# Half of a value projection moved from before attention into its filler steps, with the split weights in three rotating places

## What is computed

```python
h = x + 0.5 * swiglu(rmsnorm(x, g_ffn1), w1g, w1u, w1d)     # D_FF 2816
u = rmsnorm(h, g_mix)
qa, ka, va, qb, kb, vb = split(u @ w_in)                    # 512 128 128 512 512 512 columns
qa, ka, qb, kb = rope(...)
oa = sliding window attention with sinks(qa, ka, va)        # 8 q heads, 2 kv heads, hd 64
ob = differential attention(qb, kb, vb, lam)                # 4 heads of two 64-wide maps, 128-wide values
h = h + concat(oa, rmsnorm(ob, g_subln) * (1 - lam_init)) @ w_out
h = h + 0.5 * swiglu(rmsnorm(h, g_ffn2), w2g, w2u, w2d)
y = rmsnorm(h, final_norm)          # new keys and values are outputs too
```

## Time and profile before

| | |
|---|---|
| three runs | 1102.89, 1105.26, 1105.74 us; median 1105.26 |
| the profiled execution | 1108.34 us, its span 1106.5 us |
| TensorE | busy 97% of the span, 7890 products, mean granted clock 0.987 |
| VectorE, ScalarE, GpSimd | 62%, 43%, 8% |
| value projection | 422.8 to 458.0 us, 240 products |
| attention with fillers | 458 to some 675 us |

### The profile page before, as it was taken

How to read it: one execution, slowest core, us unless ns; L and a number is a source line. 1 busy time by engine, 2 the same in 40 slices (tenths; PEclk the granted TensorE clock), 3 DMA queues, 4 the chain that set the end, 5 groups by cost and what they waited for, 6 DMA issues and landing times. The chain is left out here.

```text
span 1106.5 us, 19039 instructions
## 1 busy us (share of the span) xinstructions
PE 1075.0 (97%) x7890; PEld 1043.7 (94%) x7890; DVE 689.4 (62%) x1083; ACT 475.1 (43%) x817; POOL 87.3 (8%) x84
## 2 busy tenths in 40 slices
PE   9999999999999999999999898999999999999996
PEld 8999999999999999877788778999999999999996
DVE  6898742488874333556678765599872268886323
ACT  6536521265653233333335443454552135655222
POOL 0000000000000213022222102100000000000112
PEclk9999999999999999989999998999999999999998
DMA  5233223223222224300111211132322323222202
GB/s 203 77 119 111 77 82 97 99 87 115 77 79 86 85 98 144 128 21 1 49 60 56 86 43 58 58 123 88 102 80 80 102 77 115 77 103 79 79 27 86
DMA packets 22660, 94.43 MB, mean 85 GB/s; under 512 B 2928, under 2 KB 6000, under 8 KB 18096
## 3 DMA queue, kind: packets, MB, share of 16 engines
q1 hardware_dynamic: 22576, 93.23, 25.0%
HBM read 88.24 MB, written 4.98 MB: 84 GB/s over the span
## 5 line engine op out<-in xcount | busy, mean ns | idle before, releaser
L1458 DVE TENSOR_TENSOR w_lo<-raw,w_hi 128x1024 fp32r<-128x1024 f32 (+3 forms) x145 | 177.1, 1221 | 208.4 <-ACT w_hi L1086 208.1
L750 PE MATMUL acc<-c_hi,w_lo 128*128 128x288 f32 x952 | 282.0, 296 | 0.0
L750 PE MATMUL acc<-c_hi,w_hi 128*128 128x288 f32 x952 | 280.9, 295 | 0.0
L750 PE MATMUL acc<-c_lo,w_hi 128*128 128x288 f32 x952 | 277.6, 292 | 0.0
L670 PE MATMUL acc<-h_hi,w_hi 128*128 128x288 f32 x1024 | 222.2, 296 | 1.0 <-DVE w_lo L1458 1.0
L670 PE MATMUL acc<-h_lo,w_hi 128*128 128x288 f32 x1024 | 221.1, 295 | 0.0
L670 PE MATMUL acc<-h_hi,w_lo 128*128 128x288 f32 x1024 | 221.0, 295 | 0.0
L1086 ACT ACTIVATE w_hi<-raw 128x1024 fp32r<-128x1024 f32 (+3 forms) x145 | 149.1, 1028 | 166.1 <-PE acc L670 147.8
L750 PEld LDWEIGHTS acc<-c_lo,w_hi 128*128 128x128 f32 x952 | 180.8, 190 | 0.0
L750 PEld LDWEIGHTS acc<-c_hi,w_hi 128*128 128x128 f32 x952 | 178.9, 188 | 0.0
L750 PEld LDWEIGHTS acc<-c_hi,w_lo 128*128 128x128 f32 x952 | 178.5, 187 | 0.0
(11 more groups left out here) (207 smaller groups left out, 1300.9 us busy)
## 6 DMA issues: line engine op xcount, KB each, us to landing
raw<-in_w1gu SPq DMA_DIRECT2D x17, 1024.0 KB, 4.8
raw<-in_w2gu SPq DMA_DIRECT2D x17, 1024.0 KB, 4.8
raw<-in_w1d SPq DMA_DIRECT2D x16, 704.0 KB, 4.0
raw<-in_w2d SPq DMA_DIRECT2D x16, 704.0 KB, 4.1
raw<-in_w_qk SPq DMA_DIRECT2D x13, 512.0 KB, 3.6
raw<-in_w1gu SPq DMA_DIRECT2D x10, 512.0 KB, 4.2
raw<-in_w2gu SPq DMA_DIRECT2D x10, 512.0 KB, 3.7
raw<-in_w_out SPq DMA_DIRECT2D x8, 512.0 KB, 4.1
```

The lines of the kernel that those rows point to most:

```text
L750: m = nc.tensor.matmul(acc[:, banks[side(f)], 0:HALF], w_part[:, col:col + P], x_part[:, k, c, :], start=n in (P1, P5, P2) and k == 0 and ...
L1458: return nc.vector.tensor_tensor(cols, src, hi.bitcast(FP32), ALU.subtract).then_inc(split_ready, 1)
```

## The change

The second half of the value projection leaves its place ahead of attention. It becomes 20 filler steps (`VALUES`, `value_step`) of two rows' blocks, six products of 320 columns each, placed in the list of fillers behind the sixth tile (kb0) and ahead of the seventh. Its token tiles alternate between banks 0 and 1; its first step waits for the take-out of the sixth tile, its third to fifth token tile for the eviction two before, and the seventh tile's first step for all ten evictions. The first scores wait for the first half's five. The loads and splits follow: the third tile comes directly behind the first two value blocks, and the other two value blocks behind the sixth tile (`FIRST_BLOCKS`, `MIDDLE`). In `w_hi` and `w_lo`, three places that begin at 0, 1280 and 2560 take turns throughout this part and in the plain gate and up blocks; the down blocks keep their two. The stores of new values move behind the eleventh tile's load. ScalarE evicts the second half in the course of the list. The lists of the order are new.

```diff
@@ -61,20 +61,23 @@
 LEAD = 2
 FILL_START = (4, 2)
-FILL = ((0, 3), (1, 2), (1, 0), (1, 1), (3, 1), (1, 0), (1, 0), (1, 1), (0, 0), (1, 3), (2, 0), (1, 0), (2, 1), (0, 2), (0, 3), (1, 2), (1, 1), (3, 0), (2, 2), (1, 0), (0, 3), (0, 5), (1, 2), (0, 5), (2, 1), (0, 5), (0, 3), (2, 3), (0, 2), (1, 4), (0, 0), (2, 2), (2, 1), (1, 0), (3, 1), (0, 3), (1, 0), (4, 0), (2, 1), (1, 12))
-ACT_SPLITS = (0, 0, 1, 0, 0, 0, 2, 1, 1, 3, 2, 0, 0, 3, 0, 5)
-DVE_SPLITS = (1, 8, 3, 4, 1, 2, 8, 3, 3, 4, 5, 0, 6, 5, 0, 2)
+FILL = ((0, 3), (0, 2), (2, 0), (1, 1), (1, 4), (0, 0), (1, 0), (1, 0), (2, 1), (3, 4), (2, 1), (3, 1), (2, 1), (2, 2), (0, 6), (2, 3), (2, 2), (4, 1), (1, 2), (2, 0), (0, 3), (0, 5), (1, 2), (0, 4), (3, 1), (0, 5), (0, 3), (2, 4), (0, 1), (1, 4), (0, 1), (2, 1), (2, 1), (1, 0), (3, 0), (1, 3), (1, 0), (4, 0), (2, 2), (1, 12))
+ACT_SPLITS = (0, 0, 1, 3, 0, 0, 1, 1, 5, 1, 1, 1, 3, 0, 1, 2, 1, 6)
+DVE_SPLITS = (1, 8, 3, 5, 0, 4, 3, 1, 5, 6, 3, 4, 6, 0, 9, 8, 1, 2)
 ACT_ROOTS = (0, 0, 0, 0)
 DVE_ROOTS = (1, 0, 0, 0)
-ROOT_ROUNDS = (1, 1, 1, 1)
-HEAD_ROUNDS = (2, 2, 4, 3)
-SCORES_FIRST = (0, 13, 16, 17, 19)
+ROOT_ROUNDS = (1, 1, 1, 3)
+HEAD_ROUNDS = (2, 2, 3, 4)
+SCORES_FIRST = (0, 7)
 V_BLOCKS = 4
 FIRST_TILES = 2
-FIRST_BLOCKS = [("qk", b) for b in range(FIRST_TILES)] + [("v", c) for c in range(V_BLOCKS)]
+FIRST_BLOCKS = [("qk", 0), ("qk", 1), ("v", 0), ("v", 1), ("qk", 2)]
+VALUES_AT = 5
+MIDDLE = [("qk", b) for b in range(FIRST_TILES + 1, len(TILES))]
+MIDDLE[VALUES_AT - FIRST_TILES:VALUES_AT - FIRST_TILES] = [("v", 2), ("v", 3)]
 def make_counts():
@@ -114,10 +117,11 @@
 FFN1_UNITS = UNIT[("qk", 0)]
-SPLIT_X, SPLIT_Y, SPLIT_Z = 0, 2176, 1024
-GENERIC = FIRST_BLOCKS + [("qk", b) for b in range(FIRST_TILES, len(TILES))]
+SPLIT_X, SPLIT_Y, SPLIT_Z = 0, 1280, 2560
+DOWN_X, DOWN_Y = 0, 2176
+GENERIC = FIRST_BLOCKS + MIDDLE
 GENERIC += [(half, p) for half in ("oa", "ob") for p in range(KH)] + [("gu", 1, 0, 0), ("gu", 1, 0, 1), ("gu", 1, 1, 0)]
 THREE_FROM = len(FIRST_BLOCKS)
@@ -126,10 +130,12 @@
     kind = key[0]
     if kind == "gu":
-        return (SPLIT_Y, SPLIT_Z, SPLIT_X)[(2 * key[2] + key[3]) % 3]
-    if kind in ("oa", "ob") or kind == "qk" and key[1] >= FIRST_TILES:
-        return (SPLIT_X, SPLIT_Y, SPLIT_Z)[(GENERIC.index(key) - THREE_FROM) % 3]
-    return (SPLIT_X, SPLIT_Y)[key[-1] % 2]
+        return (SPLIT_Z, SPLIT_X, SPLIT_Y)[(2 * key[2] + key[3]) % 3]
+    if kind == "dn":
+        return (DOWN_X, DOWN_Y)[key[3] % 2]
+    if key in FIRST_BLOCKS:
+        return (SPLIT_X, SPLIT_Z, SPLIT_X, SPLIT_Y, SPLIT_Z)[FIRST_BLOCKS.index(key)]
+    return (SPLIT_X, SPLIT_Y, SPLIT_Z)[(GENERIC.index(key) - THREE_FROM) % 3]
 def split_free(key):
@@ -147,12 +153,11 @@
         if d < 2:
             return UNIT[("st", ffn, CHUNK_F * (c + 1) - 1)] + (3, PARTS)[d]
         return UNIT[("dn", ffn, c, d - 2)] + 1
-    if kind == "v":
-        return UNIT[("v" if key[1] >= 2 else "qk", key[1] % 2 if key[1] < 4 else 0)] + 1
-    if kind == "qk" and key[1] < FIRST_TILES:
-        return UNIT[("dn", 0, 1, KD - 2 + key[1])] + 1
+    if key in FIRST_BLOCKS:
+        former = (("dn", 0, 1, KD - 2), ("dn", 0, 1, KD - 1), ("qk", 0), ("dn", 0, 1, KD - 1), ("qk", 1))
+        return UNIT[former[FIRST_BLOCKS.index(key)]] + 1
     n = GENERIC.index(key) - THREE_FROM
-    return UNIT[GENERIC[THREE_FROM + n - 3] if n >= 3 else ("v", (2, 3, 2)[n])] + 1
+    return UNIT[GENERIC[THREE_FROM + n - 3] if n >= 3 else (("v", 0), ("v", 1), ("qk", 2))[n]] + 1
 def two_on(key):
@@ -160,9 +165,13 @@
     return GENERIC[GENERIC.index(key) + 2]
-FILLERS = [(b, k) for b in range(len(TILES) + KH) for k in range(KD)]
+VALUES = -1
+VALUE_STEPS = 4 * TOK_TILES
+FILLERS = [(b, k) for b in range(VALUES_AT + 1) for k in range(KD)]
+FILLERS += [(VALUES, k) for k in range(VALUE_STEPS)]
+FILLERS += [(b, k) for b in range(VALUES_AT + 1, len(TILES) + KH) for k in range(KD)]
 LAST_FILLER = len(TILES) + KH
-OA_FROM, OB_FROM = len(TILES) * KD, len(FILLERS)
+OA_FROM, OB_FROM = FILLERS.index((len(TILES), 0)), len(FILLERS)
 FILLERS += [(LAST_FILLER, k) for k in range(KH)]
@@ -259,23 +268,32 @@
...
+def filler_key(b):
+    if b < len(TILES):
+        return "qk", b
+    return ("ob", 0) if b == LAST_FILLER else ("oa", b - len(TILES))
...
+        first = e[0] == "k" and e[2] == 0
...
+            due = {VALUES: (1,), VALUES_AT + 1: (1, 2)}.get(e[1], (2,))
+            owed += [[GENERIC[at + n], left.pop(0)] for n in due]
...
@@ -606,18 +624,18 @@
...
+            for key in FIRST_BLOCKS[3:5]:
...
-                if b == 6:
+            sp.dma_start(k_all_a[:, 0:A_PAST], a["k_past_a"]).then_inc(cache_in, 16)
+            sp.dma_start(v_past_a[:], a["v_past_a"]).then_inc(cache_in, 16)
+            for key in MIDDLE[0:1]:
+                load_first(key)
+            sp.dma_start(k_all_b[:, :, 0:PAST], a["k_past_b"]).then_inc(cache_in, 16)
+            sp.dma_start(v_past_b[:], a["v_past_b"]).then_inc(cache_in, 16)
+            for key in MIDDLE[1:]:
+                load_first(key)
+                b = key[1] if key[0] == "qk" else 0
+                if b == 10:
...
                     sp.wait_ge(v_out, 2 * TOK_TILES)
@@ -845,8 +863,10 @@
                         pe.wait_ge(res_ready, KD)
                     elif b == 2:
-                        pe.wait_ge(v_out, TOK_TILES + V_BANK.index(0) + 1)
+                        pe.wait_ge(v_out, V_BANK.index(0) + 1)
                     elif b > 2:
+                        if b == VALUES_AT + 1:
+                            pe.wait_ge(v_out, 2 * TOK_TILES)
                         pe.wait_ge(x_out, b)
                 if b == 0:
@@ -854,6 +874,16 @@
...
+            def value_products(c, tt, bank, k):
+                n_tok = P if tt < SEQ_TILES else DEC
+                tok = slice(tt * P, tt * P + n_tok)
+                col = split_base(("v", 2 * c + k // V_K)) + k % V_K * V_HALF
+                for n, (x_part, w_part) in enumerate(((u_hi, w_hi), (u_hi, w_lo), (u_lo, w_hi))):
+                    m = nc.tensor.matmul(acc[0:n_tok, bank, 0:V_HALF], x_part[:, k, tok], w_part[:, col:col + V_HALF],
+                                         start=k == 0 and n == 0, stop=k == KD - 1 and n == 2)
+                return m
...
@@ -864,33 +894,42 @@
...
+            for kc in range(2):
+                key = ("v", kc)
+                block_ready(key)
+                for tt in range(TOK_TILES):
+                    n_tok = P if tt < SEQ_TILES else DEC
+                    if kc == 0:
+                        if V_BANK[tt] == V_SUM_BANK:
+                            pe.wait_ge(r_ready, 2)
+                        elif V_BANK[tt] == 0:
+                            pe.wait_ge(x_out, 1)
+                    for k in range(V_K):
+                        m = value_products(0, tt, V_BANK[tt], V_K * kc + k)
+                    if kc == 1 and tt < TOK_TILES - 1:
+                        m.then_inc(v_done, 1)
+                m.then_inc(block_used, 1)
+            def value_step(step):
+                tt, k = step // KH, step % KH * 2
+                bank = tt % 2
+                if step == 0:
+                    block_ready(("v", 3))
+                    pe.wait_ge(x_out, VALUES_AT + 1)
+                elif k == 0 and tt >= 2:
+                    pe.wait_ge(v_out, TOK_TILES + tt - 1)
+                value_products(1, tt, bank, k)
+                m = value_products(1, tt, bank, k + 1)
+                if step == VALUE_STEPS - 1:
+                    m.then_inc(block_used, 2)
+                elif k == KD - 2:
+                    m.then_inc(v_done, 1)
...
@@ -901,7 +940,7 @@
                 pe.wait_ge(rope_done, max(TILES.index(x) for x in names) + 1)
                 wait_scores_banks(pe, n)
                 if n == 0:
-                    pe.wait_ge(v_out, 2 * TOK_TILES)
+                    pe.wait_ge(v_out, TOK_TILES)
                 if kind in ("As", "Bs"):
                     pe.wait_ge(cache_in, 64)
                 if kind == "A":
@@ -1279,29 +1320,25 @@
...
+            def value_out(c, tt):
+                n_tok = P if tt < SEQ_TILES else DEC
+                if tt < TOK_TILES - 1:
+                    act.wait_ge(v_done, (TOK_TILES - 1) * c + tt + 1)
+                else:
+                    act.wait_ge(block_used, UNIT[("v", 2 * c + 1)] + 1)
+                act.wait_ge(col_done, 4)
+                nc.scalar.activation(v_new[0:n_tok, tt, c * V_HALF:(c + 1) * V_HALF],
+                                     acc[0:n_tok, tt % 2 if c else V_BANK[tt], 0:V_HALF], ACT.Copy,
+                                     scale=r_col[0:n_tok, 1, tt:tt + 1]).then_inc(v_out, 1)
+            hi_block(("qk", 2))
+            nc.scalar.preload_act_table_set("natural_log_exp_and_others")
+            act.wait_ge(lam_sums, 2)
+            nc.scalar.activation(lam[:, 2:4], lam[:, 0:2], ACT.Exp).then_inc(lam_exp, 1)
+            hi_block(("qk", 3))
+            for tt in range(TOK_TILES):
+                value_out(0, tt)
...
@@ -1400,8 +1437,10 @@
...
```

(44 more changed lines are left out.)

54 lines of the change are left out of this document (removed).

## The result

The changed kernel takes 1108.09 us (median of 20 runs, 1105.08 to 1110.91) against 1105.43 us of the kernel before beside it (20 runs). The ratio is 1.0025, with a 95% interval of 1.0018 to 1.0033: slower by 2.8 us. That is clear of the noise of 20 runs a side, though under the 3.3 us that the prediction had set as what can be told from no change; it is 0.1 us above the top of the predicted range and 3.8 above the forecast itself. The profiled execution took 1109.23 us around a span of 1107.4.

A forecast was written before the change was run, and what follows sets the result against it. TensorE, busy 97% of the span, was taken as the bound, so only gaps and low clock could be won. -17.6 + 17.6 - 6.8 + 5.3 + 0.5 = -1.0 us from 1105.26 gave 1104.3 us, 8-in-10 range 1099.0 to 1108.0.

The forecast's parts named there:

- The moved products: Second-half value products: 17.6 us leave the place ahead of attention and return as 20 fillers of 0.88 us; balance 0.
- the split places: Three places of 1280 columns instead of uneven ones: no change in the count of instructions, costed at 0.
- (a): First value step waits for VectorE's take-out of the sixth tile, behind maxima and a wide split: 1.9 us, bounds 0 and 3.4.
- Waits that go: Sliding-window waits of 0.62, 1.63, 0.24 and 0.98 us go, 1.7 us of low clock too, 1.58 changes shape: 6.8 us together.
- (b): Seventh tile waits for the last value eviction, behind exponentials on ScalarE: 0.7 us, bounds 0 and 2.6.
- (c): Eighth tile follows the seventh with nothing between, where a transpose stood before: a wait of 1.7 us for 1.58.
- (d): Rounds 1 and 5 lose the step between transposes and values: waits of 0.35 + 0.65 = 1.0 us.
- In the differential part the steps between scores are nearly the same: Differential heads: some normalising and maxima exchanged, last head with one step and one wait less; costed at 0.
- Small terms: 63 runs of fillers against 59, about 0.1 us per change between plain and split products: 0.5 us; splits and evictions covered.
- no new wait opens: Rival: moved steps fill the gaps, VectorE having caught up at each joint: -6.3 us, 1099.0 us; chance 0.28.
- the new joints pull the clock down: Rival: three new waits each followed by a 1.2 GHz stretch of 1.7 us: +4.1 us, 1109.4 us; chance 0.16.
- the change leaves the largest early gaps alone: Rival: the two largest early gaps, at 469.30 and 488.57, are out of the change's reach; already in the sum.

The follow-up runs named there:

- e9: Changed kernel with round 9's scores moved behind the sixth tile's last step and the second wide block's split ahead of them; 1103.76 us, ratio 0.9992.
- e1: Changed kernel with the old lists of the kernel before from round 18 on (differential part); 1106.27 us, ratio 1.0011.
- e3: Changed kernel with the split of the second wide value block placed earlier on ScalarE and VectorE; 1111.69 us, ratio 1.0056.
- e10: Changed kernel with the edits of e8 and e1 together, the joint at the value steps left as it is; 1106.55 us, ratio 1.0030.
- e2: Kernel before, with the new lists from round 18 on (differential part); 1106.57 us, ratio 1.0011.
- e11: e9 with the edits of e1, and the eighth tile's first step behind round 16's values; 1101.80 us, ratio 0.9976 to the kernel before.
- e12: e11 with the edit of e4 and one ScalarE split place changed; 1099.20 us, ratio 0.9960 to the kernel before.
- e4: Kernel before, with the second scores moved behind the first transposes; 1103.93 us, ratio 0.9986.
- e7: e4 with two fillers added ahead of the first transposes and ScalarE's split of the fifth tile one place later; 1106.07 us, ratio 1.0001 to the kernel before.
- e8: e4 with the fourth tile's last step one round earlier and one ScalarE split one place later; 1105.48 us, ratio 1.0012 to the kernel before.
- e5: Changed kernel with the sixth tile finished one round earlier and the split between its take-out and the normalising; 1109.15 us, ratio 1.0034 to the kernel before.
- e6: Changed kernel with the edits of e5, e7 and e1, and one step of round 1 moved ahead of its values; 1110.29 us, ratio 1.0042 to the kernel before.

## Why the prediction was wrong

*The moved products, the loads, the split places:* right. The first scores came 18.03 us earlier, the 2.23 and 2.15 us stay, no load is late, and the second feed-forward part, which has the new split places too, takes the same time (410.4 us from its first wait, at 696.98 after, to the end, before and after). The split at (a) took 1.48 us, as the prediction had it and not the 2.10 beside a rope; a rope add of that shape takes 1.27 to 1.29 us by itself in the kernel before, so the 2.44 of the earlier trace rows had indeed grown. The split places were never run by themselves: a 1280-wide value block doesn't fit the old third place, so the old places can't carry the new order.

*Waits that go:* right; all four are gone, and the fall of the clock at 513.9 with them.

*Waits that come:* (b) 0.66 for 0.7, (c) 1.62 for 1.7, (d) 0.25 + 0.58 for 1.0. **(a) failed in size.** It was walked to 1.9 us and measured 2.97, and the walk gave it no fall of the clock, which cost 1.7 more behind it at 500.5: 4.7 us instead of 1.9, of which e9 took 4.0 away and left a wait of 0.57. All four traces with this wait at 2.9 us or more (the changed kernel, e1, e3, e10) have that fall. The prediction named VectorE's three pieces in the right order, maxima, split and take-out, but had VectorE reach them sooner than it did; it came from the normalising without a pause. How the walk came to 1.9 is not shown. The range of 0 to 3.4 held the wait itself, and had no term for the clock.

*"In the differential part the steps between scores are nearly the same [...]: 0."* **This step failed.** It measured 1.2 to 1.6 us by e1 and e2, and the part grew by 2.05 in the trace of the changed kernel, just past the 2 us at which the prediction had called itself "wrong altogether". Nearly the same numbers of steps in another order, with the next scores after the normalising instead of before it, are not the same schedule. It was a whole group of edits costed in one line, in a stretch as long as all the rest. The rows it was read from stop at 538.85: the waits of 1.61 and 1.11 us in the differential part of the kernel before (last section) are not among "the others" that the prediction counts.

*Small terms:* the gaps of the timeline sum to 10.0 us in the sliding-window part before and 11.0 after; 1.7 us less go to the clock; and the part is 0.44 longer than what moved in. 1.1 us are therefore the changes between kinds of product (and the value step's own start), where 0.5 was put.

*The clock:* the two traces differ by just the credited 1.7 us (10.2 to 8.5), but that is luck. The fall at 513.9 went, as forecast; the new ones at 500.5 and 626 took 3.4 back; and the first and last places were half as long as before, 3.4 less, which nobody forecast and which e2 shows to differ from one execution to the next. Over the runs the mean granted clock is 0.990 for both kernels: the fall behind (a) took up the credit.

The sum with the terms as measured, over many runs: -1.0 forecast, +1.7 for the clock's fall behind (a), +1.1 for the wait of (a), -0.3 for (b) to (d), +0.6 for the small terms, -0.4 for the scores' start (18.03 us earlier for 17.6), +1.2 to 1.6 for the differential part: 2.9 to 3.3. The runs say 2.8. Some of these terms come from one trace each, so the agreement is closer than they deserve. One sum of the prediction does not come out either: its upper terms give -1.0 + 3.4 = +2.4, where it wrote +2.7.

*The rivals.* That no new wait opens was wrong. Part of the reserve it named was there: with room at the joints and the old order of the heads, e11 took 2.7 of its 6.3 us; the 4.4 of e12 include the edit of e4, which the kernel before could have too. That the new joints pull the clock down was right for one of three; (b) and (c) had no low place behind them. Its sign, more low places than four, showed (five), though one of the five, at 626, is at no new joint. That the change leaves the largest early gaps alone is true, and e7 and e8 show that they don't close by moving fillers to them.

## What to carry to other kernels

A filler that moves into a gap brings its own waits: ask which bank its first product takes, who has to empty that, and what stands before the emptying on that engine's list. When one engine's in-order list decides, move what nobody needs yet behind what somebody waits for, as e9 did with one pair of events; moving the awaited work, or what stands before it, to an earlier place (e3, e5, e8) only let something else come late. Where low stretches of the clock are worth as much as the waits, take the clock out of the runs before saying what an edit did: e4 won by the clock alone, and e5's loss was hidden by it. And when a change rewrites a hand-made order, no stretch of it costs nothing because the counts are alike: write out both orders there too, or give the term a range.

## What was not expected of the hardware

The same order gives nearly the same trace: behind the joint, e9 and the changed kernel differ by 3.94 to 4.03 us at all of 32 marks (the starts of scores and transposes) over 155 us.

The granted clock does not follow from the wait before it alone. Behind waits of 1.57 to 1.62 us on the same scores, the clock fell in the changed kernel (0.66 at 626 to 631) and stayed at 1.00 in the kernel before. With waits of 1.55 to 1.62 us there, e6, e9 and e12 have the fall too and the nine other runs have not; both lists of the differential part are among either kind, so the list does not decide it. These are single executions, and the mean clock of the changed kernel alone goes from 0.987 to 0.994 over its 20 runs; no run shows what decides. TensorE's timeline of the kernel before has there:

```profile
623.29 1.13 PE L923 MATMUL acc<-k_b,q_b 64*128 64x512 f32 x4 [1.61 <-ACT probs L1330]
...
630.66 0.60 PE L988 MATMUL acc<-v_new,probs_t 128*128 128x128 f32 x3 [1.11 <-ACT probs_t L1355]
```

Nor does a fall cost its whole 1.7 us everywhere: behind the one in the changed kernel the wait of 1.11 us shown here is missing, since the copy had time to be ready. It is missing in e6, e9 and e12 as well, and there in the others. About 0.6 us of the 1.7 is left, and that is most of the difference between the 1.50 us of e2's trace and the 2.05 in the changed kernel's.
